# A two-block transformer forward in float32: convolution products in four buffers, delta-rule gating a tile ahead, first level masked by GpSimd, third scores sooner

## The chip, the cores and the metric

The kernel runs on one core of one Trainium2 chip. The metric is the device time of one execution in microseconds (us), the median of several runs. Engine names in the text: TensorE (PE), VectorE (DVE), ScalarE (ACT), GpSimd (POOL), SyncE (SP, which here only issues the loads of weights).

## The reference

Two transformer blocks over one sequence of 512 tokens with 1024 features, all in float32. Reduced to what the change touches:

```python
# block 1, delta rule: per chunk of 64 tokens and per head
lower = b * (k k^T) * dec_strict
sol   = triangular_solve(lower + I, rhs)            # the inverse is built in levels
o     = scan(step, s0, ...)                         # state passed from chunk to chunk
ya    = rmsnorm(o, norm_w) * silu(z)                # the gating of the outputs
# block 1, sparse attention: scores against compressed blocks, selected blocks and a window
p = softmax(q k^T - slope * dist);  yb = sum of gates * (p v)
mixed = (g_a * (ya @ w_a2d) + g_b * (yb @ w_b2d)) @ w_o
# feed-forward with a short convolution, then a per-layer embedding, then block 2:
q, k, v, glu_a, glu_g = split(rms_norm(h) @ w_in)
u = glu_a * sigmoid(glu_g)
u = depthwise_conv(u, 31 taps) + b;  u = silu(layer_norm(u))
h = h + concat(attention(q, k, v), u) @ w_out
# and a second feed-forward
```

## The kernel before

**Weights.** All large products multiply a 128x128 weight block with 512 tokens. A weight arrives as float32 in `RAW[b]` (two buffers), ScalarE rounds it into `WH[b]` (`stage_hi`, L302, tile name whi), VectorE subtracts to get the low half `WL[b]` (`stage_lo`, L309, wlo), and TensorE makes three products per block, high by high, high by low and low by high (`product`, L322 to L324). A piece is up to 16 blocks, so 48 products. `stage_hi(ph, i, b)` waits until TensorE has ended the piece that lies in buffer b and then rounds the piece after the next; TensorE waits for its low half (`weights_ready`). Each engine runs its own list of instructions in the order written; semaphores tie them together. `T` is 4 tiles of 128 tokens.

**First level (gdn_pe, gdn_act, gdn_dve, gdn_pool).** Per tile t, VectorE makes the decayed key-key blocks (L994 to L999, signal `at_ready`), the query-key block (L1003, `qk_done`) and then the start of the inverse, identity minus the entries of level 0: L1005 multiplies `ATC` by the mask `level`, L1006 takes it from `eye` (`tt_ready`). GpSimd scales the queries (L1084, after `qk_done`) and masks the entries of level 1 into `OFFC[1]` (L1077); later it masks those of the levels 2 to 5 into the two buffers in turn. TensorE turns each tile (L679) when `tt_ready` says so, and five levels follow, each as products (L700), copies by ScalarE (L883), products (L708), a subtraction by VectorE (L1011) and turns.

**Gating.** After the recurrence, TensorE turns the outputs of tile t (L790) into bank 4 + t % 2, VectorE multiplies by the gain and the gate into `TMP[t % 2]` (L1067, `yt_ready`), ScalarE takes the high half (L908, `yt_hi`), VectorE the low half (L1070, `yt_lo`). TensorE goes on to the next turn when `yt_ready` of the tile before is there, and, after the last turn and one more such wait, to the rest of the projection "nq".

**Scores of block 1 (nsa_pe, nsa_dve).** A pair p of heads goes through scores on TensorE (L1219), `top(p)` on VectorE (bias and maximum, L1380), the exponential on ScalarE (L1338), `factors(p)` on VectorE (L1388, L1389), scaling on GpSimd (L1467), turn, copy and values on TensorE. Pairs 0 and 1 are started ahead of the value projection `nv_pe` (L1132 to L1134); then the compressed scores (L1264) follow, and the loop over `ITER` starts with pair 2.

**Convolution of block 2 (blk2_act, blk2_dve, conv_pool).** 31 taps for each of four channel groups. VectorE sums 73 of the taps (`TAPS`, L2065 and L2068), the other 51 (`LATE_TAPS`) are multiplied by ScalarE (L1986 for a group's first, L1989 for the rest) into a buffer of `PT2` and added by GpSimd (L2199, `last_tap_done`). ScalarE's product k waits for the add of product k - 2, as there are two buffers. This runs beside the projections "glu" (four pieces), "qk2" (four) and "v2" (two): ScalarE does a gate (L1997), a `stage_hi` and five products for each group, then six products and a `stage_hi` for each piece of "qk2", then the rest, then the exponentials. GpSimd scales the probabilities (L2207) after its last add. The tile `PT2` has four parts of 512 columns, of which the products use two.

```python
                    else:
                        act.wait_ge(last_tap_done, k - 1)
                        ins = nc.scalar.mul(PT2[:, 0, k % 2, :], src, w)
...
            for p in range(NPIECE["qk2"]):
                products(6)
                stage_hi(act, "qk2", p // 2, p % 2, p >= 2)
```

## Time and profile before

| what | value |
|---|---|
| median of 3 runs | 1605.27 us (1605.24 to 1605.73) |
| the profiled execution: its own time | 1607.56 us |
| its span | 1605.8 us |
| mean granted clock of TensorE | 0.971 |
| TensorE busy with products | 1529.8 us, 95% |
| VectorE busy | 867.0 us, 54% |
| ScalarE busy | 641.9 us, 40% |
| GpSimd busy | 212.6 us, 13% |

The span is the part of the execution that the profile covers; the time of the same execution is 1.76 us longer, and it is 2.3 us above the median of the other runs. Times in the rows are microseconds from the start of the span, unless marked ns. A granted clock of 1.00 is 2.4 GHz, 0.50 is 1.2 GHz. Products are pipelined, so that one starts about 0.23 us after the one before it although each is listed with 0.39 us.

### The profile page before, as it was taken

To read this page: it belongs to the slowest core of one execution; us is meant where nothing else is said; L and a number is where in the kernel's file an instruction comes from. 1 tells how busy PE (TensorE), PEld (TensorE's weight loads), DVE (VectorE), ACT (ScalarE), POOL (GpSimd) and SP (SyncE) were. 2 spreads that over 40 slices of the span, in tenths; PEclk is the share of its full clock that TensorE was granted. 3 is DMA by queue.
4 is the path that set the end of the run, shared out by engine and by line. 5 is a ranking of instruction groups with operands and counts; after the bars stand their busy time and mean duration, and the time that the engine had idled before them with its cause. 6 is when DMAs were issued, how large, how long until landed. Compare 5 with 4: busy or idle time off the path is not lost. (4 is left out here: it accounts for less than half of the span.)

```text
span 1605.8 us, 21770 instructions
## 1 busy us (share of the span) xinstructions
PE 1529.8 (95%) x8438; PEld 1247.9 (78%) x8438; DVE 867.0 (54%) x1300; ACT 641.9 (40%) x936; POOL 212.6 (13%) x191
## 2 busy tenths in 40 slices
PE   6997999999999899999999998989799999999998
PEld 5777978667888777888888876767578888888886
DVE  5755446673444477766732266677626444444222
ACT  5354422463223244443422155454635444443221
POOL 0004000681000000000000001378610000000000
PEclk9999999999999999999999998999979999999999
DMA  5210032001223313233232233122103223222321
GB/s 211 79 53 16 2 142 101 21 1 40 98 93 110 105 53 103 81 104 104 69 115 90 91 123 105 53 79 79 30 24 105 91 92 104 99 83 73 104 94 71
DMA packets 22534, 132.17 MB, mean 82 GB/s; under 512 B 2480, under 2 KB 2864, under 8 KB 12224
## 3 DMA queue, kind: packets, MB, share of 16 engines
q1 hardware_dynamic: 20672, 123.48, 22.8%
q0 software_dynamic: 928, 6.36, 1.0%
q10 hardware_dynamic: 864, 1.36, 0.2%
q8 instruction: 49, 0.80, 0.2%
q14 instruction: 21, 0.17, 0.0%
HBM read 129.09 MB, written 2.10 MB: 82 GB/s over the span
## 5 line engine op out<-in xcount | busy, mean ns | idle before, releaser
L322 PE MATMUL ps<-AH,whi 128*128 128x512 f32 x1280 | 509.6, 398 | 39.1 <-DVE wlo L309 14.6
L323 PE MATMUL ps<-AL,whi 128*128 128x512 f32 x1280 | 504.8, 394 | 0.0
L324 PE MATMUL ps<-AH,wlo 128*128 128x512 f32 x1280 | 504.3, 394 | 0.0
L309 DVE TENSOR_TENSOR wlo<-raw,whi 128x2048 fp32r<-128x2048 f32 (+3 forms) x124 | 251.2, 2026 | 272.0 <-ACT whi L302 271.8
L322 PEld LDWEIGHTS ps<-AH,whi 128*128 128x128 f32 x1280 | 244.7, 191 | 95.9 <-issue 21.9
L324 PEld LDWEIGHTS ps<-AH,wlo 128*128 128x128 f32 x1280 | 244.3, 191 | 52.0
L323 PEld LDWEIGHTS ps<-AL,whi 128*128 128x128 f32 x1280 | 244.5, 191 | 50.4 <-issue 0.2
L302 ACT ACTIVATE whi<-raw 128x2048 fp32r<-128x2048 f32 (+3 forms) x124 | 210.3, 1696 | 169.9 <-PE ps L324 169.9
L322 PE MATMUL ps<-HH,whi 128*128 128x512 f32 x352 | 136.9, 389 | 0.0
L323 PE MATMUL ps<-HL,whi 128*128 128x512 f32 x352 | 136.9, 389 | 0.0
L324 PE MATMUL ps<-HH,wlo 128*128 128x512 f32 x352 | 136.9, 389 | 0.0
L322 PEld LDWEIGHTS ps<-HH,whi 128*128 128x128 f32 x352 | 66.1, 188 | 13.8
L323 PEld LDWEIGHTS ps<-HL,whi 128*128 128x128 f32 x352 | 66.1, 188 | 13.7
L324 PEld LDWEIGHTS ps<-HH,wlo 128*128 128x128 f32 x352 | 66.1, 188 | 13.6
L2199 POOL TENSOR_TENSOR CU<-CU,PT 128x512 f32<-128x512 f32 x49 | 74.4, 1519 | 15.7 <-ACT PT L1989 9.8
L1467 POOL TENSOR_SCALAR PR<-PR,RL 128x384 f32<-128x384 f32 (+3 forms) x60 | 63.3, 1071 | 12.8 <-DVE RL L1389 12.4
L2246 POOL TENSOR_TENSOR hT<-CG,RR 128x512 f32<-128x512 f32 x2 | 2.5, 1264 | 426.5 <-ACT RR L2241 426.5
L2317 POOL DMA_DIRECT2D XF<-pT x1 | 0.8, 769 | 433.9 <-PE ps L324 433.9
L329 PE MATMUL ps<-ident,PR 128*128 128x128 f32 x224 | 40.6, 302 | 9.1 <-ACT PT L1975 5.2
L1989 ACT ACTIVATE PT<-UG,cols 128x512 f32<-128x512 f32 x49 | 34.5, 719 | 34.8 <-POOL CU L2199 34.8
L329 PEld LDWEIGHTS ps<-ident,PR 128*128 128x128 f32 x224 | 25.3, 147 | 29.2 <-issue 13.8
L2068 DVE SCALAR_TENSOR_TENSOR ps<-UG,cols,ps 128x512 f32<-128x512 f32 x67 | 47.6, 747 | 0.5
(384 smaller groups left out, 1928.9 us busy)
## 6 DMA issues: line engine op xcount, KB each, us to landing
raw<-wstream SPq DMA_DIRECT2D x78, 1024.0 KB, 4.8
raw<-wstream SPq DMA_DIRECT2D x32, 704.0 KB, 4.1
raw<-wstream SPq DMA_DIRECT2D x16, 768.0 KB, 4.3
hT<-xT SPq DMA_DIRECT2D x4, 512.0 KB, 7.9
raw<-wstream SPq DMA_DIRECT2D x4, 512.0 KB, 3.6
W1k<-w1k_d POOLq DMA_DIRECT2D x1, 2048.0 KB, 10.7
W1v<-w1v_d POOLq DMA_DIRECT2D x1, 2048.0 KB, 15.9
BT<-bias_d POOLq DMA_DIRECT2D x1, 1024.0 KB, 5.6
```

The lines of the kernel that those rows point to most:

```text
L302: nc.scalar.activation(WH[b][:, 0:n], RAW[b][:, 0:n], ACT.Copy).then_inc(w_hi_done, 1)
L309: nc.vector.tensor_tensor(WL[b][:, 0:n], RAW[b][:, 0:n], WH[b][:, 0:n].bitcast(F32), ALU.subtract).then_inc(w_lo_done, 1)
L322: nc.tensor.matmul(out_, WH[b][:, w], xh[:, k, :], start=start and k == 0, stop=False)
L323: nc.tensor.matmul(out_, WH[b][:, w], xl[:, k, :], start=False, stop=False)
L324: last = nc.tensor.matmul(out_, WL[b][:, w], xh[:, k, :], start=False, stop=stop and k == n - 1)
L329: return nc.tensor.transpose(out_, x, eye)
L1467: nc.gpsimd.tensor_scalar(x, x, RL[:, p % 4, b:b + 1], None, ALU.mult).then_inc(p_scaled, 1)
L1989: ins = nc.scalar.mul(PT2[:, 0, k % 2, :], src, w)
L2068: ins = vec.scalar_tensor_tensor(to, src, w, acc(c), ALU.mult, ALU.add)
L2199: nc.gpsimd.tensor_tensor(CU[:, c, :], CU[:, c, :], PT2[:, 0, k % 2, :], ALU.add).then_inc(last_tap_done, 1)
L2246: nc.gpsimd.tensor_tensor(hT[:, m, :], OUT_TMP[n], RR[:, :], ALU.mult).then_inc(out_pooled, 1)
L2317: pool.dma_start(PX, pT.rearrange("(c p) s -> p c s", p=P)).then_inc(p_landed, 16)
```

## The change

Four things are changed.

1. Convolution: the products of ScalarE go into four buffers in turn, product k waits for the add of product k - 4; three, seven, six and four products follow the four gates instead of five each; in "qk2" the rounding comes before the six products instead of behind them.
2. First level: GpSimd masks level 0 into `OFFC[0]` as well, ahead of level 1 and of the scaling of the queries, as soon as `at_ready` is there. VectorE makes one subtraction, `eye` minus `OFFC[0]`, a tile later (`first_level`). Counts of `off_ready` move by four; the masks of level 2, which overwrite `OFFC[0]`, wait for `tt_ready`.
3. Gating: VectorE's gate of tile t + 1 is put ahead of the low half of tile t. TensorE does not wait for `yt_ready` after the last turn.
4. Third scores: `scores(2)` is put ahead of the compressed scores, `factors(1)` behind `factors(0)`, and `top(2)` ahead of the low half of the weights of "mix".

```diff
--- before.py
+++ after.py
@@ -692,7 +692,7 @@
             for lev in range(1, LEVELS - 1):
                 for t in range(T):
                     n = 4 * lev + t
-                    pe.wait_ge(off_ready, n - 3)
+                    pe.wait_ge(off_ready, 2 * t + 2 if lev == 1 else n + 1)
                     pe.wait_ge(t_ready, n - 3)
                     pe.wait_ge(tt_ready, n - 3)
                     for h in range(GH):
@@ -736,7 +736,7 @@
                 last.then_inc(kv_ps, 1)
 
             pe.wait_ge(t_ready, 4 * (LEVELS - 1) + 2)
-            pe.wait_ge(off_ready, 4 * (LEVELS - 2) + 1)
+            pe.wait_ge(off_ready, 4 * (LEVELS - 1) + 1)
             for t in range(T):
                 pe.wait_ge(kv_sb, t + 1)
                 for h in range(GH):
@@ -789,7 +789,7 @@
                 for h in range(GH):
                     last = turned(ps[:, 4 + t % 2, h * P:(h + 1) * P], AT[:, t, h, :], ident[:, :])
                 last.then_inc(ot_ps, 1)
-                if t >= 1:
+                if 0 < t < T - 1:
                     pe.wait_ge(yt_ready, t)
 
 
@@ -883,7 +883,7 @@
                     nc.scalar.activation(flat(YC[b, t, :, :]), ps[b, t, 0:GH * HB], ACT.Copy).then_inc(y_sb, 1)
                 if lev < LEVELS - 1:
                     save_t(lev)
-            act.wait_ge(off_ready, 4 * (LEVELS - 2))
+            act.wait_ge(off_ready, 4 * (LEVELS - 1))
             for n, b in enumerate(halves):
                 nc.scalar.activation(TT[b, :, :, n * HB:(n + 1) * HB].rearrange("p t h n -> p (t h) n"),
                                      TTC[b, :, :, :].rearrange("p t h n -> p (t h) n"), ACT.Copy).then_inc(t_ready, 1)
@@ -968,7 +968,12 @@
             dve.wait_ge(gsum_done, 1)
             vec.tensor_copy(flat(GC[:, :, :]), ps[:, 7, 0:16]).then_inc(gc_saved, 1)
             dve.wait_ge(gc_saved, 1)
-            level, eye = (CS[:, CON[x]:CON[x] + HB].unsqueeze(1).to_broadcast([P, GH, HB]) for x in ("level", "eye"))
+            eye = CS[:, CON["eye"]:CON["eye"] + HB].unsqueeze(1).to_broadcast([P, GH, HB])
+
+            def first_level(t):
+                dve.wait_ge(off_ready, 2 * t + 1)
+                vec.tensor_tensor(TTC[:, t, :, :], eye, OFFC[0][:, t, :, :], ALU.subtract).then_inc(tt_ready, 1)
+
             sums = lambda bank: ps[:, bank, :].rearrange("p (t h n) -> p t h n", t=T, h=GH)[:, :, :, 0]
             lo, hi = halves
 
@@ -1001,9 +1006,9 @@
                     decay(t + 2)
                 dve.wait_ge(rows_done, 4 * t + 4)
                 vec.tensor_tensor(flat(QK[:, t, :, :]), ps[:, o + 3, :], flat(QK[:, t, :, :]), ALU.mult).then_inc(qk_done, 1)
-                dve.wait_ge(at_ready, t + 1)
-                own.link(vec.tensor_tensor(TTC[:, t, :, :], ATC[:, t, :, :], level, ALU.mult))
-                vec.scalar_tensor_tensor(TTC[:, t, :, :], TTC[:, t, :, :], -1.0, eye, ALU.mult, ALU.add).then_inc(tt_ready, 1)
+                if t:
+                    first_level(t - 1)
+            first_level(T - 1)
             for lev in range(1, LEVELS - 1):
                 for t in range(T):
                     n = 4 * lev + t
@@ -1058,36 +1063,45 @@
                                   ALU.mult).then_inc(on_ready, 1)
             stage_lo(dve, "z", 0, 1, True)
             dve.wait_ge(z_ready, 4)
+            def output(t):
+                dve.wait_ge(ot_ps, t + 1)
+                vec.scalar_tensor_tensor(TMP[:, t % 2, :].rearrange("p (h n) -> p h n", h=GH),
+                                         ps[:, 4 + t % 2, :].rearrange("p (h n) -> p h n", h=GH), col("gdn"),
+                                         ZS[:, :, t * P:(t + 1) * P], ALU.mult, ALU.mult).then_inc(yt_ready, 1)
+
+            output(0)
             for t in range(T):
+                if t + 1 < T:
+                    if t:
+                        dve.wait_ge(yt_lo, t)
+                    output(t + 1)
+                dve.wait_ge(yt_hi, t + 1)
                 tok = slice(t * P, (t + 1) * P)
-                dve.wait_ge(ot_ps, t + 1)
-                tmp = TMP[:, t % 2, :].rearrange("p (h n) -> p h n", h=GH)
-                if t >= 2:
-                    dve.wait_ge(yt_lo, t - 1)
-                vec.scalar_tensor_tensor(tmp, ps[:, 4 + t % 2, :].rearrange("p (h n) -> p h n", h=GH), col("gdn"),
-                                         ZS[:, :, tok], ALU.mult, ALU.mult).then_inc(yt_ready, 1)
-                dve.wait_ge(yt_hi, t + 1)
-                vec.tensor_tensor(YAL[:, :, tok], tmp, YAH[:, :, tok].bitcast(F32), ALU.subtract).then_inc(yt_lo, 1)
+                vec.tensor_tensor(YAL[:, :, tok], TMP[:, t % 2, :].rearrange("p (h n) -> p h n", h=GH),
+                                  YAH[:, :, tok].bitcast(F32), ALU.subtract).then_inc(yt_lo, 1)
 
         def gdn_pool(pool):
             def offs(lev, t):
                 m = CS[:, CON["level"] + lev * HB:CON["level"] + (lev + 1) * HB].unsqueeze(1).to_broadcast([P, GH, HB])
+                if lev == 2:
+                    pool.wait_ge(tt_ready, t + 1)
                 if lev > 2:
                     pool.wait_ge(y_ps, 4 * (lev - 3) + t + 1)
                 nc.gpsimd.tensor_tensor(OFFC[lev % 2][:, t, :, :], ATC[:, t, :, :], m, ALU.mult).then_inc(off_ready, 1)
 
             nc.gpsimd.memset(ST[:, :, :, :], 0.0).then_inc(state_ready, 1)
             for t in range(T):
+                pool.wait_ge(at_ready, t + 1)
+                offs(0, t)
+                offs(1, t)
                 qd = QKV[:, 0:GH, t * P:(t + 1) * P]
                 pool.wait_ge(row_exp, t + 1)
                 pool.wait_ge(qk_done, t + 1)
                 nc.gpsimd.tensor_tensor(qd, qd, Y1[:, t, :, :], ALU.mult).then_inc(qd_ready, 1)
-                pool.wait_ge(at_ready, t + 1)
-                offs(1, t)
             for lev in range(2, LEVELS - 1):
                 for t in range(T):
                     offs(lev, t)
-            pool.wait_ge(off_ready, 4 * (LEVELS - 2))
+            pool.wait_ge(off_ready, 4 * (LEVELS - 1))
             nc.gpsimd.memset(TT[halves[1], :, :, 0:HB].rearrange("p t h n -> p (t h) n"), 0.0).then_inc(off_ready, 1)
 
 
@@ -1296,10 +1310,11 @@
                                                 W2[:, 2 + f, :], start=f == 0, stop=f == 1)
             last.then_inc(kv_c_ps, 1)
             nv_pe(pe, 1)
+            scores(2)
             pe.wait_ge(kv_c_sb, 1)
             compressed_scores()
             for i in ITER:
-                if i < len(PAIRS):
+                if 2 < i < len(PAIRS):
                     scores(i)
                 if i - 2 < len(PAIRS):
                     turn(i - 2)
@@ -1412,6 +1427,7 @@
             top(1)
             nv_dve(dve, 0)
             factors(0)
+            factors(1)
             dve.wait_ge(kv_c_ps, 1)
             for g in range(NG):
                 for b in range(2):
@@ -1421,11 +1437,12 @@
                                           ps[32 * r:32 * r + NC, 6, (1 + g) * DK:(2 + g) * DK])
             ins.then_inc(kv_c_sb, 1)
             nv_dve(dve, 1)
+            top(2)
             stage2_lo(dve, "nv", 1)
             for i in ITER:
-                if i - 1 < len(PAIRS):
+                if 2 < i < len(PAIRS) + 1:
                     factors(i - 1)
-                if i < len(PAIRS):
+                if 2 < i < len(PAIRS):
                     top(i)
                 if i - 2 < len(PAIRS) and i not in ACT_SAVES_BOTH:
                     save_probs(dve, vec.tensor_copy, i - 2, 0)
@@ -1985,8 +2002,9 @@
                         act.wait_ge(ug_ready, c + 1)
                         ins = nc.scalar.activation(CU[:, c, :], src, ACT.Identity, bias=B2[:, c:c + 1], scale=w)
                     else:
-                        act.wait_ge(last_tap_done, k - 1)
-                        ins = nc.scalar.mul(PT2[:, 0, k % 2, :], src, w)
+                        if k >= 4:
+                            act.wait_ge(last_tap_done, k - 3)
+                        ins = nc.scalar.mul(PT2[:, k // 2 % 2, k % 2, :], src, w)
                     ins.then_inc(prod_ready, 1)
                 del left[:n]
 
@@ -1997,10 +2015,10 @@
                 nc.scalar.activation(SQ[:, b, :], SQ[:, b, :], ACT.Tanh, scale=0.5).then_inc(gate_ready, 1)
                 if c:
                     stage_hi(act, "glu", i, b, i == 1)
-                products(5)
+                products((3, 7, 6, 4)[c])
             for p in range(NPIECE["qk2"]):
+                stage_hi(act, "qk2", p // 2, p % 2, p >= 2)
                 products(6)
-                stage_hi(act, "qk2", p // 2, p % 2, p >= 2)
             products(len(LATE_TAPS))
 
             def probabilities(p):
@@ -2196,7 +2214,7 @@
                 pool.wait_ge(prod_ready, k + 1)
                 if j:
                     pool.wait_ge(last_tap_done, k)
-                    nc.gpsimd.tensor_tensor(CU[:, c, :], CU[:, c, :], PT2[:, 0, k % 2, :], ALU.add).then_inc(last_tap_done, 1)
+                    nc.gpsimd.tensor_tensor(CU[:, c, :], CU[:, c, :], PT2[:, k // 2 % 2, k % 2, :], ALU.add).then_inc(last_tap_done, 1)
                 else:
                     nc.gpsimd.memset(B2[:, c:c + 1], 0.0).then_inc(last_tap_done, 1)
             for p in range(len(PAIRS2)):
```

## Rows read from the trace of the kernel before

**Rows 1.** The page, engines: busy time, share of the span.

```profile
PE 1529.8 (95%) x8438; PEld 1247.9 (78%) x8438; DVE 867.0 (54%) x1300; ACT 641.9 (40%) x936; POOL 212.6 (13%) x191
```

**Rows 2.** Groups by line, 112 to 134: busy us, mean ns, idle before.

```profile
L1006 DVE SCALAR_TENSOR_TENSOR Tm<-Tm,CS 128x256 f32<-128x256 f32 x4 | 5.5, 1376 | 0.1
L1084 POOL TENSOR_TENSOR QKV<-QKV,Y 128x512 f32<-128x512 f32 x4 | 5.2, 1312 | 123.3 <-DVE QK L1003 123.3
L1077 POOL TENSOR_TENSOR OFF<-TT,CS 128x256 f32<-128x256 f32 x5 | 4.3, 864 | 0.0
...
L1005 DVE TENSOR_TENSOR Tm<-TT,CS 128x256 f32<-128x256 f32 x4 | 1.6, 408 | 0.0
```

**Rows 3.** Timelines, 130 to 134: start us, us, instruction, [idle before <- releaser].

```profile
130.99 1.97 PE L679 MATMUL ps<-ident,Tm 64*64 64x64 f32 x32 [5.98 <-DVE AT L999]
133.43 1.12 PE L679 MATMUL ps<-ident,Tm 64*64 64x64 f32 x16 [0.46 <-DVE Tm L1006]
...
131.91 1.38 DVE L1006 SCALAR_TENSOR_TENSOR Tm<-Tm,CS 128x256 f32<-128x256 f32 x1
...
131.69 1.31 POOL L1084 TENSOR_TENSOR QKV<-QKV,Y 128x512 f32<-128x512 f32 x1 [2.08 <-DVE QK L1003]
```

**Rows 4.** Timeline of TensorE, the gating and the product after it.

```profile
216.74 1.04 PE L329 MATMUL ps<-ident,AT 128*128 128x128 f32 x8
...
222.35 0.80 PE L322 MATMUL ps<-AH,whi 128*128 128x512 f32 x1 [1.39 <-DVE TMP L1067]
```

**Rows 5.** Timeline of VectorE, first gate and last low half.

```profile
217.45 0.75 DVE L1067 SCALAR_TENSOR_TENSOR TMP<-ps,cols,ZS 128x512 f32<-128x512 f32 x1 [1.70 <-PE ps L329]
...
225.04 0.69 DVE L1070 TENSOR_TENSOR YAL<-TMP,YAH 128x512 fp32r<-128x512 f32 x1 [0.69 <-ACT YAH L908]
```

**Rows 6.** Windows of 1 us: length, TensorE busy (count), granted clock, DMA share, GB/s.

```profile
221.00:222.00 1.00, 0.00 (x0) 0.50 0.00 0
...
227.00:228.00 1.00, 1.00 (x4) 0.60 0.47 111
```

**Rows 7.** Timeline of TensorE around the third scores.

```profile
289.41 4.12 PE L1264 MATMUL ps<-KC,QT 64*128 64x32 f32 x64
293.34 2.06 PE L1219 MATMUL ps<-KT,QT 64*128 64x512 f32 x4
...
301.38 1.13 PE L1219 MATMUL ps<-KT,QT 64*128 64x512 f32 x4
```

**Rows 8.** Groups by line, the convolution's stretch, 1023 to 1118.

```profile
L2199 POOL TENSOR_TENSOR CU<-CU,PT 128x512 f32<-128x512 f32 x49 | 74.4, 1519 | 15.7 <-ACT PT L1989 9.8
L2068 DVE SCALAR_TENSOR_TENSOR ps<-UG,cols,ps 128x512 f32<-128x512 f32 x58 | 40.8, 747 | 0.5
...
L309 DVE TENSOR_TENSOR wlo<-raw,whi 128x2048 fp32r<-128x2048 f32 x7 | 16.4, 2343 | 13.2 <-ACT whi L302 13.2
L302 ACT ACTIVATE whi<-raw 128x2048 fp32r<-128x2048 f32 x7 | 13.3, 1901 | 0.0
...
L2085 DVE TENSOR_TENSOR TMP<-ps,RR 128x512 f32<-128x512 f32 x4 | 2.7, 683 | 0.1
```

**Rows 9.** Timeline of TensorE: a whole piece, and the two waits for weights.

```profile
1023.56 0.44 PE L322 MATMUL ps<-AH,whi 128*128 128x512 f32 x1
...
1034.32 0.39 PE L324 MATMUL ps<-AH,wlo 128*128 128x512 f32 x1
1036.51 0.61 PE L322 MATMUL ps<-AH,whi 128*128 128x512 f32 x1 [1.81 <-DVE wlo L309]
...
1077.66 0.79 PE L322 MATMUL ps<-AH,whi 128*128 128x512 f32 x1 [6.37 <-DVE wlo L309]
```

**Rows 10.** Timelines: an add beside a subtraction, the last adds, scores 2.

```profile
1034.82 2.77 POOL L2199 TENSOR_TENSOR CU<-CU,PT 128x512 f32<-128x512 f32 x1 [0.54 <-ACT PT L1989]
...
1106.40 11.53 POOL L2199 TENSOR_TENSOR CU<-CU,PT 128x512 f32<-128x512 f32 x7 [0.38 <-ACT PT L1989]
...
1127.20 1.99 PE L1866 MATMUL ps<-KT,QT 64*128 64x512 f32 x8 [0.63 <-DVE V L2113]
```

## The prediction

> **What bounds the kernel now.** I read the page first. Its top says that TensorE is busy for 95% of the span [rows 1], so time can come only from three things: stretches in which TensorE stands still, stretches in which it runs at the lower of its two clock levels, and work taken off it. The change takes no matrix product away, so I looked for standstills and slow stretches next to the edited lines, with the timeline of TensorE, the list of grouped instructions of two stretches, and 1 us windows for the granted clock.
>
> Four places stand out. In the first level of the triangular inverse TensorE waits 5.98 us and then 0.46 us for VectorE [rows 3]. In the gating of the delta rule's output it waits 1.39 us before each of the last steps, and starts the next projection at half clock [rows 4, 6]. At the third scores it runs slowly without waiting [rows 7]. In the convolution it waits 1.81 us and 6.37 us for the low half of weights, both times followed by slow products [rows 9].
>
> **The port.** Before pricing anything I needed to know why L1006 is so slow. L1005 and L1006 have the same 128x256 shape, but one takes 408 ns and the other 1376 ns [rows 2]. At the last tile GpSimd's L1084 runs 131.69 to 133.00 and L1006, started at 131.91, ends at 133.29, just behind it [rows 3]: a VectorE operation that reads two SBUF tensors stands still while a GpSimd operation runs. The reverse shows in the convolution: an add that starts at 1034.82, during the weight subtraction L309, takes 2.77 us [rows 10], where others in the 49 give a pace of about 1.30 + 0.14 us; the 49 average 1519 ns because of it [rows 8]. The Trainium skill says the same of the two engines (SBUF — State Buffer, "Who interferes with whom": a VectorE instruction with two SBUF inputs contends with a GpSimd instruction that reads SBUF, and who starts first keeps the port for the whole instruction). The trace agrees, and its waits are in the terms below.
>
> **First level masked by GpSimd.** Removed from VectorE: four L1005 (0.41 each, 0.44 to the next start) and four L1006 at 1.38, in steps of 1.30 [rows 2]: 4 x 1.74 = 7.0 us. Added: four subtractions of 256 columns; the nearest row is L1005, so 4 x 0.44 = 1.8 us. They read two SBUF tensors, so each can be held by GpSimd. The first is not (it stands right behind the operation that frees GpSimd's next one); the other three come while a mask of their own or the next tile is running, whose length is at most 0.86 us [rows 2]. I take 0.3, 0.3 and 0.6, together 1.2. TensorE is late once (the decay rows of tile 3, because VectorE is now earlier): 0.3 us. Net: 7.0 - 1.8 - 1.2 - 0.3 = 3.7; with the last subtraction waiting only for a mask that is half done it is 4.1. I take 3.9 us; bounds 3.0 (all three held for 0.86) and 4.9 (none held). All of it is on the path: the last tile's turn at 133.43 follows L1006's end by 0.14 us [rows 3]. GpSimd gets four more masks, 4 x 0.86 = 3.5 us, before the last L1084. ScalarE's first copy of a level waits for that L1084; I get its end at about 130.5; the copy needs the level's first products, which follow the turn now at 133.43 by about 2 us, so they come at about 131.5: hidden by 1 us. The clock is no loss: it falls during the long wait and would fall again.
>
> The Trainium skill speaks against this edit (GPSIMD Engine Reference, "Engine selection": elementwise work belongs on VectorE, as GpSimd is about twice as slow with two inputs). The rows agree on the price: 864 ns for a GpSimd mask (part of it waiting) against 408 ns [rows 2]. By that rule the four masks cost 1.8 us more than before; by the rows the extra is on an engine that waits anyway, and the term stays.
>
> **Gating a tile ahead.** Now the loop is a chain: gate on VectorE (0.75), high half on ScalarE, low half on VectorE, next gate; four tiles take 8.3 us [rows 5], and TensorE's turn of tile 3 and then the projection hang on it. After: gates 0 and 1 run back to back, 217.45 to about 218.9, turn 3 needs only gate 1, and no wait on gate 2 follows. The turn runs 218.9 to 219.5 and the projection starts at 219.5 instead of 222.35 [rows 4]: 2.85 us. VectorE ends its last low half at about 223.0 instead of 225.73. Queued behind it are the query copies and the weight subtraction that the next but one piece needs at 236; they are due at 225.6, early enough. GpSimd's loads of the compression weights wait for the last low half, so they also start 2.7 us sooner; TensorE needs them only past 250, no cost.
>
> Then the clock. The stretch from the turns at 216.74 to 222.35 is sparse, the level drops to 0.5 in 221-222 and stays there until 227.6 [rows 6]. Twelve products at 0.43 us instead of 0.23 us (steps in rows 9) lost 2.5 us. With dense work from 219.5, before the point at which the level dropped, I expect it not to drop. Gain 2.5, bounds 0 and 2.5. Together 5.35 us.
>
> **Third scores sooner.** TensorE has no wait here: 64 narrow products in 4.12 us, then scores at half clock, 2.06 us against 1.13 us later at full clock [rows 7]. Moved in front of the narrow ones, behind the dense value projection, the scores run in 1.1 us: 0.9 us less. But the slow stretch begins with the sparse products, which now come later, and it then covers other work of the same density: what is saved at its front may be lost at its end. VectorE's order changes too: factors(1) and top(2) come ahead of a weight subtraction. That weight subtraction queued behind top(2) is 1.3 us later, but is needed only for the mixing gate 80 us on. GpSimd gets pair 1's scaling earlier. I take 0.4 us, bounds -0.5 and 1.5.
>
> **The convolution.** Here three things are chained: ScalarE rounds weights (1.90) and makes products; VectorE subtracts the low half (2.34), reads banks (0.68 a read) and sums taps (747 ns each, in steps of about 0.67, or 0.79 where each needs the one before); GpSimd adds [rows 8]. A TensorE piece of 48 products takes 11.0 us (1023.56 to 1034.32 for 47 steps) [rows 9].
> Step 1. ScalarE does three products instead of five before the second gate, none waiting for an add, so that gate and the rounding come 2.8 us earlier; the low half is done at 1033.7, before TensorE ends its piece at 1034.7. The 1.81 us wait is gone, and the slow start (1.8 us).
> Step 2. From one low half to the next there are then 8 taps (5.4; 6.3 in the first), two bank reads 1.3, the gate on ScalarE, which I estimate at 0.75, the rounding 1.85 and the subtraction 2.2: 11.5 us (12.4 in the first) against 11.0. The low halves come at 1033.7, 1046.0 and 1057.4, where TensorE is ready at 1034.6, 1045.5 and 1057.0: two waits of about 0.5 us.
> Step 3. For the first query piece rounding no longer stands behind six products that each wait for an add (the 6.37 us wait); it is done at 1059.5. What is late next is VectorE, with 8 taps, two copies and four taps: low half done about 1069.2, TensorE ready at 1068.4. Wait 0.9 us. The piece starts at 1069.3 instead of 1077.66, at full clock, which saves another 1.7 us. The later pieces don't wait.
> The sum at the first scores: 1.8 + 1.8 + 6.4 + 1.7, less new waits 0.5 + 0.5 + 0.9, is 9.8; worked step by step it is 10.1. I take 10.1: scores at 1102.1 instead of 1112.2.
> Step 4. GpSimd ends its adds at 1106.40 + 11.53 = 1117.93 now [rows 10]; it stood idle 9.8 us for want of a product [rows 8]. After, I count about 4 us, so 5.6 less, but the subtractions now find it busy and some adds wait 0.4 us longer, four of them: the last add ends at about 1114.0. Scaling of pair 0 (3.1 us) follows to 1117.1. TensorE is ready for that pair's turn at 1115.4, and waits 1.7 us that it doesn't wait now. Scores 2 start at 1118.2 instead of 1127.20 [rows 10]: 9.0. For the chance of a slow stretch after this wait I take 0.4 off: 8.6 us. Bounds: 6.0 (the four subtractions that TensorE waits for held for a whole add, 4 x 0.65 more than half an add) and 10.1 (adds done in time).
> Fresh buffers cost nothing: the other half of that tile is idle here.
>
> **Sum.** 3.9 + 5.35 + 0.4 + 8.6 = 18.25 us. The profiled execution's span was 1605.8 and its time 1607.56, so 1.76 lies around the span: after, 1587.55 and 1589.3. It stands 2.3 us above the median of the runs, so the median goes from 1605.27 to 1587.0.
>
> **Rivals.**
> 1. The clock falls in the gating in spite of the shorter gap, since two short waits remain there: 2.5 us less gained, 1589.5. For it: at 1036.51 a wait of 1.81 us was enough for a slow start [rows 9]. Against: dense work now comes 1.5 us before the drop. 15%.
> 2. The convolution gives back more: GpSimd's adds are held by every subtraction and end at 1117.9 as now; scaling and turn take 4.2 us more, so scores 2 come at 1122.5. Gain there 4.7 less 0.4: 1591.3. 12%.
> 3. GpSimd bounds the first level: per tile two masks, one L1084 and a held subtraction, 0.86 x 2 + 1.31 + 0.44 = 3.5 us against VectorE's 3.2; three tiles, 0.9 us less: 1587.9. Hardly to be told from mine in time, only in the trace. 10%. (The rule of the Trainium skill's GPSIMD Engine Reference quoted above leads here.)
> 4. Slower than before. With rounding ahead of the products ScalarE waits for TensorE's piece (11 us) with at most four products out, 5.7 us of adds: GpSimd may idle 5 us in each of six pieces. Scores 2 would have to come at 1137, after a last add at 1132, to eat the other 9.65 us too; it decides from 18 us of idleness beyond my 4 on. Against: the products that ScalarE makes between two roundings are six, 8.6 us of adds, so a piece leaves 2.4 us idle, not 5. 3%.
> 5. The edits do nothing because other waits take over at once: 1605. 2%.
> The rest, 58%, is my own case, 1584.5 to 1589.5.
>
> **How the numbers follow.** What can be told from no change here is 0.2%, 3.2 us. Only rivals 4 and 5 don't end beyond it: faster 0.95, same 0.02, slower 0.03. Sum of the bounds in the good direction is 1583 (4.9 + 5.35 + 1.5 + 10.1 = 21.9); rival 2 with most of rival 1 is 1593. Range 1583.5 to 1593.
>
> **What would show it.** No 1.8 and 6.4 us waits before L322 in the convolution; its query piece 3 starting 8.4 us sooner after the same start; a new wait of TensorE for GpSimd's scaling before the first turn. The new subtraction ending 3.7 to 4.1 us sooner in the first level, its duration over 0.42 us where it was held. Full clock behind the gating. Wrong would be: a wait in the first level for ScalarE's copy behind L1084, a clock drop behind the gating, or adds that end past 1116 (counted with this stage's shift taken off).

## The result, and the profile after

The changed kernel takes 1582.53 us (median of 4 runs, 1581.71 to 1585.38), the kernel before 1605.5 us beside it: the ratio is 0.9858, 95% interval 0.9841 to 0.9875. I had predicted 1587.0 with a range from 1583.5 to 1593.0, so the kernel is 1 us faster than the fast end of the range. Its profiled execution took 1582.03 us with a span of 1580.2; against the profiled one of before that is 25.5 us, where the sum was 18.25.

Top of the page after, engines first and then the granted clock in 40 slices. TensorE's busy time fell by 11.8 us against [rows 1] though no product was removed: it ran less at the lower level.

```profile
PE 1518.0 (96%) x8438; PEld 1239.6 (78%) x8438; DVE 863.9 (55%) x1296; ACT 641.0 (41%) x936; POOL 217.1 (14%) x195
...
PEclk9999999999999899999999998999889999999999
```

**First level.** Timelines of VectorE, TensorE and GpSimd after, beside [rows 3]. All starts are shifted by about 0.6 us from the loads at the start on.

```profile
122.18 0.41 DVE L975 TENSOR_TENSOR Tm<-CS,OFF 128x256 f32<-128x256 f32 x1
...
125.03 0.56 DVE L975 TENSOR_TENSOR Tm<-CS,OFF 128x256 f32<-128x256 f32 x1
...
128.02 1.43 DVE L975 TENSOR_TENSOR Tm<-CS,OFF 128x256 f32<-128x256 f32 x2
...
127.55 0.69 PE L679 MATMUL ps<-ident,Tm 64*64 64x64 f32 x8 [3.47 <-DVE AT L1004]
...
127.58 1.59 POOL L1090 TENSOR_TENSOR OFF<-TT,CS 128x256 f32<-128x256 f32 x2 [0.19 <-DVE AT L1004]
129.13 1.45 POOL L1100 TENSOR_TENSOR QKV<-QKV,Y 128x512 f32<-128x512 f32 x1
```

The wait of 5.98 us is 3.47 us, the second one of 0.46 is gone. The four subtractions took 0.41, 0.56, 0.56 and 0.94 us (the last two are one line above), where an unheld one takes 0.41. The last three each end 0.27 to 0.29 us behind the end of a GpSimd mask: they are held, and only a little. GpSimd still waits for VectorE (0.19 us), so it doesn't bound the level. The Trainium skill says that a VectorE instruction with two SBUF inputs contends with a GpSimd instruction that reads SBUF (SBUF — State Buffer, "Who interferes with whom"); the trace agrees, with 0.15, 0.15 and 0.53 us as the price here.

**Gating.** Timeline of TensorE, then 1 us windows with all engines (the column behind POOL is the granted clock), beside [rows 4, 6].

```profile
214.11 1.31 PE L329 MATMUL ps<-ident,AT 128*128 128x128 f32 x8 [0.48 <-DVE TMP L1068]
215.19 0.48 PE L322 MATMUL ps<-AH,whi 128*128 128x512 f32 x1
```

```profile
216.00:217.00 1.00, 1.00 (x6) 0.84 (x5) 0.96 (x3) 0.63 (x1) 0.00 (x0) 1.00 0.00 0
...
222.00:223.00 1.00, 1.00 (x7) 0.81 (x6) 0.00 (x0) 0.00 (x0) 0.70 (x2) 1.00 0.82 193
```

One wait of 0.48 us is left, the projection starts with a product of 0.48 us instead of 0.80, and the clock stays at 1.00.

**Third scores.** Timeline of TensorE and 2 us windows, beside [rows 7].

```profile
279.69 1.13 PE L1233 MATMUL ps<-KT,QT 64*128 64x512 f32 x4
280.65 3.66 PE L1278 MATMUL ps<-KC,QT 64*128 64x32 f32 x64
...
285.26 1.13 PE L1233 MATMUL ps<-KT,QT 64*128 64x512 f32 x4
...
289.94 0.63 PE L329 MATMUL ps<-ident,PR 128*128 128x128 f32 x4 [0.44 <-ACT PT L1342]
```

```profile
284.00:286.00 2.00, 2.00 (x18) 1.35 (x16) 1.60 (x3) 1.06 (x2) 0.00 (x0) 1.00 0.52 80
```

No group runs at the lower level any more: the scores take 1.13 us both times, the narrow products 3.66 instead of 4.12.

**Convolution.** Timelines of TensorE and GpSimd, then GpSimd's and ScalarE's groups from 1007 to 1103, beside [rows 8 to 10].

```profile
1030.71 0.50 PE L322 MATMUL ps<-AH,whi 128*128 128x512 f32 x1 [0.26 <-DVE wlo L309]
1053.97 0.50 PE L322 MATMUL ps<-AH,whi 128*128 128x512 f32 x1 [0.76 <-DVE wlo L309]
...
1100.74 0.63 PE L329 MATMUL ps<-ident,PR 128*128 128x128 f32 x4 [0.35 <-POOL PR L2225]
1102.19 0.66 PE L329 MATMUL ps<-ident,PR 128*128 128x128 f32 x4 [0.82 <-POOL PR L2225]
...
1078.73 20.32 POOL L2217 TENSOR_TENSOR CU<-CU,PT 128x512 f32<-128x512 f32 x13 [0.17 <-ACT PT L2007]
1099.03 3.11 POOL L2225 TENSOR_SCALAR PR<-PR,RL 128x512 f32<-128x512 f32 x2
```

```profile
L2217 POOL TENSOR_TENSOR CU<-CU,PT 128x512 f32<-128x512 f32 x49 | 76.3, 1556 | 10.1 <-ACT PT L2007 3.9
...
L2007 ACT ACTIVATE PT<-UG,cols 128x512 f32<-128x512 f32 x49 | 33.4, 716 | 18.4 <-POOL CU L2217 18.2
```

The waits of 1.81 and 6.37 us are gone; 0.26 and 0.76 us stand in their place. GpSimd's adds end at 1099.05; with the 15.1 us by which the stage starts sooner, that is 1114.2 (forecast 1114.0). TensorE's new waits for its scaling (L2225) are there, 1.2 us together (forecast 1.7).

### The profile page after: what moved, and what is told of

The parts are those of the page before. It is cut to its first block and busy times, and to the rows that moved or that the text cites. A ratio compares the mean times of both kernels' runs of the same rounds, so it can differ in the third digit from the quotient of the medians.

```text
span 1580.2 us, 21770 instructions
## 1 busy us (share of the span) xinstructions
PE 1518.0 (96%) x8438; PEld 1239.6 (78%) x8438; DVE 863.9 (55%) x1296; ACT 641.0 (41%) x936; POOL 217.1 (14%) x195
## 5 line engine op out<-in xcount | busy, mean ns | idle before, releaser
L322 PEld LDWEIGHTS ps<-AH,whi 128*128 128x128 f32 x1280 | 242.7, 190 | 85.9 <-issue 21.4
L2217 POOL TENSOR_TENSOR CU<-CU,PT 128x512 f32<-128x512 f32 x49 | 76.3, 1556 | 10.1 <-ACT PT L2007 3.9
L1353 ACT ACTIVATE PR<-ps,NM 128x384 f32<-128x384 f32 (+3 forms) x60 | 30.5, 513 | 27.3 <-DVE NM L1395 27.2
```

What stands on the lines that cost most here:

```text
L322: nc.tensor.matmul(out_, WH[b][:, w], xh[:, k, :], start=start and k == 0, stop=False)
L1353: nc.scalar.activation(probs(p, b)[:, 0:n], ps[:, u % 4, 0:n], ACT.Exp, bias=NM[:, u % 4, :], scale=-1.0, accum_out=LS[:, p % 4, b:b + 1]) ...
L2217: nc.gpsimd.tensor_tensor(CU[:, c, :], CU[:, c, :], PT2[:, k // 2 % 2, k % 2, :], ALU.add).then_inc(last_tap_done, 1)
```

## The experiments

Where an experiment's trace gains or loses is read from one difference: the start of an instruction there less the start of the same instruction in the trace of before. The table gives how this difference changes over seven stretches (named by before's times) and its value at the end; below 0 is sooner. The last columns are the runs.

| kernel | 110-140 | 216-230 | 230-288 | 288-330 | 370-380 | 1007-1127 | 1127-1200 | end | median, us (runs) | before beside it |
|---|---|---|---|---|---|---|---|---|---|---|
| changed | -3.85 | -5.63 | +0.05 | -2.59 | -2.47 | -9.16 | -1.40 | -25.8 | 1582.53 (4) | 1605.50 |
| a_again, the same | -4.21 | -5.63 | 0.00 | -2.58 | -2.50 | -9.13 | -1.53 | -27.6 | 1585.75 (4) | 1607.28 |
| a_more, the same | -4.06 | -5.62 | +0.03 | -2.59 | -0.87 | -9.07 | -1.17 | -24.0 | 1585.41 (4) | 1607.41 |
| a_last, the same | -4.25 | -5.62 | +1.59 | -2.58 | -0.90 | -9.08 | -1.20 | -24.5 | 1584.76 (4) | 1606.85 |
| b_again, before | -0.05 | -1.06 | +1.66 | +1.08 | -2.49 | +1.27 | -1.61 | -2.7 | 1605.08 (1) | 1607.28 |
| s_first | -3.78 | -1.22 | +1.66 | -0.38 | +0.37 | +0.54 | +0.29 | -2.6 | 1601.52 (12) | 1606.36 |
| s_gate | -0.25 | -5.62 | +1.63 | -0.74 | -0.96 | -0.08 | +0.77 | -6.7 | 1600.81 (6) | 1606.36 |
| s_third | -0.12 | +0.27 | +0.01 | -2.55 | -2.46 | +1.19 | +0.61 | -4.5 | 1602.97 (12) | 1606.36 |
| s_conv | +0.12 | +0.24 | +0.01 | -0.22 | -2.47 | -9.17 | -1.19 | -12.9 | 1595.66 (6) | 1606.36 |
| s_order | -0.23 | +0.03 | +0.05 | +0.01 | 0.00 | -8.76 | -1.22 | -10.8 | 1596.03 (4) | 1607.28 |
| a_2buf | -4.28 | -5.62 | +1.54 | -2.59 | -0.91 | -8.67 | +0.63 | -22.0 | 1584.27 (4) | 1605.61 |
| a_nothird | -3.86 | -5.61 | +0.02 | +0.12 | -0.14 | -9.14 | -1.15 | -19.9 | 1585.59 (4) | 1607.28 |
| a_nothird2 | -4.16 | -5.62 | +1.63 | +0.48 | -0.90 | -9.28 | -0.60 | -20.7 | 1588.22 (4) | 1607.41 |
| v_pe | -4.07 | -5.62 | +0.03 | -0.76 | +0.13 | -9.32 | -0.48 | -20.1 | 1587.90 (4) | 1606.85 |
| v_dve | -4.04 | -5.62 | +1.65 | +4.05 | +0.05 | -9.31 | -0.57 | -13.4 | 1590.05 (4) | 1606.85 |
| f_glu | -3.68 | -5.62 | +1.46 | -2.58 | -0.92 | -9.10 | -1.15 | -22.6 | 1585.40 (4) | 1607.41 |
| f_att2 | -4.27 | -5.63 | +1.60 | -2.58 | -0.88 | -9.10 | -1.20 | -24.7 | 1582.11 (5) | 1607.41 |
| f_att2b | -4.08 | -5.62 | +1.59 | -2.58 | -0.88 | -9.16 | -1.03 | -23.9 | 1583.98 (5) | 1606.85 |
| f_five | -4.38 | -5.63 | +1.49 | -2.60 | -0.93 | -9.22 | -1.42 | -25.5 | 1582.15 (5) | 1605.61 |

### The four parts, each alone

Each is the kernel before with one of the four changes, the diff here in short: s_first `first_level` and GpSimd's masks of level 0; s_gate `output(t + 1)` a tile ahead and the last wait gone; s_third the moved `scores(2)`, `factors(1)`, `top(2)`; s_conv buffers and order.

```diff
 s_first: -own.link(level mask)     +first_level(t - 1)
 s_gate:  -if t >= 1:              +if 0 < t < T - 1:
 s_third: +scores(2)  (ahead of compressed_scores)
 s_conv:  -products(5)             +products((3, 7, 6, 4)[c])
```

> The kernel before with the first level's edit alone (masks of level 0 on GpSimd, VectorE only subtracts). Theory A (each part is worth its own waits and its own slow stretch, and the parts add): the wait of 5.98 us before the first level is 3.5 us and the place is left 4.5 to 4.8 us sooner; time 4.5 us below before. Theory B (what exceeded the forecast comes from slow stretches elsewhere, which depend on all shifts together): the shift at the end of the span differs from that behind the first level by 2 us or more, because a slow stretch further on comes or goes. The drop at 371 to 378 us stays in A and may go in B.

> The kernel before with the gating's order alone. Theory A: 5.4 to 5.6 us gained behind the gating (2.9 of waits, the rest because TensorE's clock no longer falls in 221 to 228), the same 5.5 us at the end; the drops at 292 to 300 and 371 to 378 us stay. Theory B: one of these two goes as well and 2.4 us or more come on top, 7.5 to 10 us in all.

> The kernel before with the third scores and their factors moved alone. Theory A: the drop at 292 to 300 us and that at 371 to 378 us both go with this edit, since they lie in the stage that it reorders: 2.5 us gained by 316 us, 4.9 to 5.0 us by 380 us and at the end. Theory B (the recorded term of 0.4 us was right for this edit alone, and the rest came with the earlier shift of the stage): 0 to 1 us gained by 316 us, the drop at 371 us stays, at most 1 us in all.

> The kernel before with the convolution's edits alone (four product buffers, rounding ahead of the products). Theory A: 9.3 us sooner at the scores of pair 2 relative to the start of the stage, 10.4 us at the end of the span with the short drop at 1132 to 1136 us gone. Theory B: in the stage the same 9.3 us, but the slow stretches behind it fall elsewhere, and the end differs from 10.4 us by 1.5 us or more, either way.

Ratios: s_first 0.9967 (0.9957 to 0.9978), s_gate 0.9960 (0.9946 to 0.9975), s_third 0.9981 (0.9972 to 0.9990), s_conv 0.9939 (0.9922 to 0.9956). The medians lie 4.8, 5.6, 3.4 and 10.7 us below before, together 24.5, beside 21.5 to 23.0 for the changed kernel in its four comparisons. So the parts add within the width of their intervals, as theory A says, and each shows its gain in its own stretch. Two expectations of theory A fell: s_third was to gain 4.9 to 5.0 us at the end and its runs gained 3.4, and s_conv ends 12.9 us sooner instead of 10.4, as B said. s_conv edits nothing ahead of 1000 us and yet is 2.47 us sooner in 370-380. Timelines of TensorE, before and then s_conv:

```profile
371.09 0.40 PE L329 MATMUL ps<-ident,PR 128*128 128x128 f32 x1 [0.30 <-POOL PR L1467]
371.42 0.70 PE L1246 MATMUL ps<-PT,V 128*64 128x128 f32 x4
...
373.54 2.08 PE L1255 MATMUL ps<-CP,VB 128*128 128x128 f32 x8
```

```profile
371.17 0.30 PE L329 MATMUL ps<-ident,PR 128*128 128x128 f32 x1 [0.30 <-POOL PR L1467]
371.40 0.44 PE L1246 MATMUL ps<-PT,V 128*64 128x128 f32 x4
...
373.22 1.16 PE L1255 MATMUL ps<-CP,VB 128*128 128x128 f32 x8
```

From 320 to 371 us both start the same instructions within 0.1 us of each other; then one falls to the lower level and the other doesn't. (Further ahead they differ by up to 1 us, since the slow stretch at 293 us is shorter in s_conv.)

### Twice the same kernel

> The kernel before once more, unchanged, for its trace. The kernel with the convolution's edit alone showed full clock at 371 to 378 us although nothing ahead of 1000 us was edited in it. Theory C: which of the slow stretches behind sparse work appear differs from one execution to the next, so that this trace differs from the first one in at least one of the stretches at 220, 292, 371, 1132 and 1190 us, with starts of instructions ahead of it that agree within 0.5 us. Theory A (a slow stretch belongs to the schedule): the same stretches, all fourteen within 1 us.

> The changed kernel once more, for a narrower interval and a second trace. Theory A: 1582.5 us, 23.8 us below before, and no slow stretch between 134 and 538 us again. Theory C: the same median within 1.5 us, but one slow stretch of those that were absent (220, 292 or 371 us, counted in the time of before) is there in this trace, or one at 1133 to 1154 us is shorter.

b_again bears out theory C. a_again doesn't by itself: its trace has none of the absent stretches, as theory A said, and its median of 1585.75 us lies 3.2 above the first one's, further than either theory allowed. But a_more has a slow stretch at 360 us, and a_last one at 237 and one at 360, that the first two traces of the changed kernel lack. Windows of 2 us in the first trace of before and then in b_again:

```profile
224.00:226.00 2.00, 2.00 (x7) 1.52 (x6) 1.31 (x3) 1.58 (x2) 0.00 (x0) 0.50 0.00 0
...
250.00:252.00 2.00, 2.00 (x11) 1.64 (x10) 1.97 (x4) 0.00 (x0) 0.00 (x0) 1.00 0.81 197
...
374.00:376.00 2.00, 2.00 (x10) 1.90 (x10) 0.00 (x0) 0.00 (x0) 0.00 (x0) 0.50 0.00 0
```

```profile
224.00:226.00 2.00, 2.00 (x9) 1.62 (x8) 2.00 (x4) 0.90 (x1) 1.02 (x2) 0.87 0.03 8
...
250.00:252.00 2.00, 2.00 (x6) 1.55 (x6) 1.97 (x4) 0.00 (x0) 0.00 (x0) 0.55 0.38 160
...
374.00:376.00 2.00, 2.00 (x14) 1.78 (x14) 0.00 (x0) 0.00 (x0) 0.00 (x0) 1.00 0.04 8
```

The slow stretch behind the gating is shorter in b_again, one at 250 is new, the one at 374 is missing. The 62 runs of the kernel before reach from 1603.4 to 1609.9 us (median 1606.5), the 16 of the changed one from 1580.2 to 1589.1 (median 1584.9). The first measurement's 1582.53 is the lowest of four medians; pooled, the change is worth 21.6 us. That the spread comes from the clock is in part argued: over the 16 runs the time falls as the mean granted clock rises (0.982 in the fastest, 0.976 in the slowest), but only one run of each set of four has a trace. The Trainium skill puts the point at which the level changes down to where the work falls in a count of the chip's own that doesn't start with the kernel (TensorE: Matmul & The Clock Gate, "What's actually happening"); the traces agree, as far as two executions with equal starts and unequal levels can show it.

### The third scores, put back and halved

a_nothird and a_nothird2 are the changed kernel without `scores(2)` ahead, `factors(1)` and `top(2)`; v_pe undoes VectorE's lines alone, v_dve TensorE's alone (each with its condition in the loop).

```diff
 v_pe:             v_dve:
-factors(1)       -scores(2)   (ahead of compressed_scores)
-top(2)
```

> The changed kernel with the third scores, factors and top put back to their place of before. Theory A (the edit keeps the clock up in its stage): a slow stretch is back at about 282 to 290 us and the time is 2.5 to 3.4 us longer than the changed kernel's, 1585 to 1586 us. Rival (the slow stretch there had gone because the gating's edit shifted the stage): no slow stretch there, and the time within 1 us of the changed kernel's.

> The changed kernel without the third scores' edit, a second time. Theory: slow stretches at about 282 to 290 us and 360 to 370 us as in its first trace, 2.5 to 5 us longer than the changed kernel. Rival: one of the two stretches is missing here, and the medians differ by less than 1.5 us.

> The changed kernel a third time, beside the same kernel without the third scores' edit, for more runs of both. Theory (the third scores' edit is worth 2.5 us and more): this kernel's median is 2.5 to 5 us below that of the kernel without it. Rival (the recorded 0.4 us, on the mean over executions): the two medians within 1.5 us. Nearly no slow stretch between 134 and 538 us in this trace under the theory; one of two traces has one under the rival.

> The changed kernel with VectorE's half of the third scores' edit undone (factors(1) and top(2) back behind the weight subtraction); TensorE still takes scores(2) ahead of the narrow products. Theory (the order on TensorE alone keeps its clock up, since the scores follow the dense value projection and the narrow products stand in their place): no slow stretch at 280 to 290 us, 2.6 us gained between 288 and 316 us of before's time, time as the changed kernel's within 1 us. Rival (VectorE's sooner factors close waits of TensorE in 286 to 294 us and that keeps it up): the slow stretch is back, and the time is 2.5 us longer.

> The changed kernel with TensorE's half of the third scores' edit undone (scores(2) back behind the narrow products); VectorE keeps its new order. Theory: the slow stretch of 6.8 us at 282 to 290 us is back and nothing is gained there, 2 to 3 us slower than the changed kernel. Rival: no slow stretch, 2.6 us gained all the same. VectorE stands at top(2) until those scores come, so the weight subtraction behind it is late by some 4 us in either case, and is needed only much later.

Timeline of TensorE in v_dve and then in v_pe:

```profile
281.83 3.76 PE L1278 MATMUL ps<-KC,QT 64*128 64x32 f32 x64
285.43 1.74 PE L1233 MATMUL ps<-KT,QT 64*128 64x512 f32 x4
...
295.70 0.60 PE L329 MATMUL ps<-ident,PR 128*128 128x128 f32 x3 [1.99 <-ACT PT L1341]
```

```profile
280.59 3.66 PE L1278 MATMUL ps<-KC,QT 64*128 64x32 f32 x64
...
285.20 1.13 PE L1233 MATMUL ps<-KT,QT 64*128 64x512 f32 x4
...
290.09 0.63 PE L329 MATMUL ps<-ident,PR 128*128 128x128 f32 x4 [0.65 <-ACT PT L1342]
```

All ten traces with the whole edit gain 2.55 to 2.60 us in 288-330, and none has a slow stretch there; all nine without TensorE's half (before's two among them) have one. v_pe has none either, and gains 2.34 us by 316, before a slow stretch at 306 to 310 us takes 1.58 back. So TensorE's order is what removes the slow stretch at the scores. In its runs, though, v_pe misses its expectation (within 1 us of the changed kernel): 1587.90 us, against 1584.76 for a_last beside it. Its slow stretch at 306 us isn't explained by waits, since those ahead of it are the same in a_more, which has none there. Window of v_pe, then the longest such wait in v_pe and in a_more:

```profile
306.00:308.00 2.00, 2.00 (x19) 1.67 (x18) 0.33 (x2) 0.60 (x3) 2.00 (x2) 0.57 0.04 8
```

```profile
304.13 0.63 PE L329 MATMUL ps<-ident,PR 128*128 128x128 f32 x4 [1.07 <-ACT PT L1342]
```

```profile
303.41 0.63 PE L329 MATMUL ps<-ident,PR 128*128 128x128 f32 x4 [1.05 <-ACT PT L1342]
```

Whether VectorE's half is worth something by itself stays open. v_dve is worse in this stretch than doing nothing: VectorE stands at `top(2)` for scores that come late, and TensorE then waits 1.99 us for probabilities and has two more slow stretches, at 296 and 313 us; it loses 4.05 us there. In time the edit is worth about 2.5 us: 1587.4 (median of 8 runs without it) against 1584.9. This is less sure than the traces: the ranges of runs overlap (1583.2 to 1589.9 and 1580.2 to 1589.1), and of the two pairs measured side by side one shows 2.8 us (a_nothird2 and a_more) and the other nothing (a_nothird 1585.59, a_again 1585.75), against the expectation of 2.5 to 3.4.

### The convolution's order and its buffers

s_order is before with the order alone and two buffers, a_2buf the changed kernel with two buffers. The diff is a_2buf's against the changed kernel, ScalarE's side; GpSimd's add reads the same part of `PT2`.

```diff
-if k >= 4:
-    act.wait_ge(last_tap_done, k - 3)
-ins = nc.scalar.mul(PT2[:, k // 2 % 2, k % 2, :], src, w)
+act.wait_ge(last_tap_done, k - 1)
+ins = nc.scalar.mul(PT2[:, 0, k % 2, :], src, w)
```

> The kernel before with the convolution's order alone (rounding ahead of the products, 3, 7, 6, 4 and 6 products), still with two product buffers. Theory (the order frees the weights, the buffers only keep the products from waiting): the waits of 1.8 and 6.4 us shrink to under 1 and under 3 us, but each product past the second waits for the add two before it, so gates and roundings are still 1 to 3 us late in each piece; 6 to 8 us gained. Rival (the buffers don't matter): 10 us gained as with both. Other rival (without the buffers the order gives nothing, since ScalarE stands behind the adds all the same): under 3 us.

> The changed kernel with two product buffers again, all else kept. Theory (the order does it, the buffers only let ScalarE run ahead): 0.1 to 0.5 us less gained at the scores of pair 2 (8.7 to 9.1 us from the start of the stage instead of 9.1 to 9.2), time within 1 us of the changed kernel's 1585. Rival (with all edits together the buffers matter): 1 us and more lost between 1007 and 1127 us of before's time.

ScalarE's and GpSimd's groups in s_order, 1007 to 1118:

```profile
L2199 POOL TENSOR_TENSOR CU<-CU,PT 128x512 f32<-128x512 f32 x49 | 75.9, 1548 | 11.0 <-ACT PT L1989 5.1
...
L1989 ACT ACTIVATE PT<-UG,cols 128x512 f32<-128x512 f32 x49 | 34.5, 719 | 35.9 <-POOL CU L2199 35.9
```

With two buffers ScalarE stands 35.9 us before its products instead of 18.4, but nothing on TensorE's path waits behind it: GpSimd's idle time before its adds is 11.0 us against 10.1. The order brings 8.76 of 9.17 us (s_conv), the buffers 0.4 to 0.5. My expectation for s_order (6 to 8 us) was too low, and the rival that the buffers don't matter is nearly right. a_2buf came within 1 us of the changed kernel.

### What a slow stretch costs

The changed kernel keeps a slow stretch of 20 us in the second attention and one of 10 to 14 us at the GLU's norm. Added products that serve nothing (their results are overwritten) fill such places.

```diff
 f_att2, f_att2b, f_five, in scores(p):
+if p >= 11 and b == 0:
+    nc.tensor.matmul(ps[:, s2_bank(p, b), :], ones[:, :], KT2[:, 0, :], start=True, stop=True)
 f_att2, f_att2b: the same once ahead of values(14) and values(15)
 f_glu, the product once ahead of spread_rms(pe, 4) and four times behind it:
+pe.wait_ge(bank_free, RING0["glu"] + 2)
+nc.tensor.matmul(ps[:, ring("glu", 0), :], ones[:, :], E[:, 0, :], start=True, stop=True)
```

> The changed kernel with seven products added that serve nothing (ones by KT2, 128x512 f32, into a scores bank that is free), one ahead of each of the scores 11 to 15 of the second attention and one ahead of the values of pairs 14 and 15. Theory (the long slow stretch of 20.5 us at 1132 to 1154 us is set by how little work TensorE gets there, and its waits leave room): the stretch is gone or at most 10 us long, the first product of the output projection starts 2 to 6 us sooner, and the kernel is 2 to 6 us faster than the changed one in spite of 6 us of added work. Rival (the waits for ScalarE and VectorE set the pace there, the clock is only a symptom): the stretch may go, but the time stays within 1.5 us. Second rival (the clock doesn't follow the work): the stretch stays and the kernel is 3 to 6 us slower.

> The changed kernel with five products added that serve nothing (ones by E, 128x512 f32), one ahead of the spreading of the root before the GLU projection and four behind it, where TensorE waits 1.1 and 3.2 us. Theory (a wait followed by dense work costs its length and a slow start; filling the wait saves the slow start): the stretch of 10.2 us at 976 to 987 us goes or shrinks to 3.4 us, the projection's products run in steps of 0.23 us from the start, 1.5 to 3 us gained. Rival (the projection's first products are paced by VectorE's low halves, so a full clock gives nothing): under 0.7 us. The added products end ahead of the first low half at 981.6 us and delay nothing in either.

> The changed kernel with the seven added products in the second attention, once more. Theory D (the slow stretch costs time in the plain executions): its median again 2 to 4 us below the changed kernel's of the same call. Theory E (as its first trace says, ScalarE's and VectorE's waits set the pace there, and the first difference was a spread between runs): within 1.5 us of it, and in the trace 1.2 us gained from 1127 to 1200 us of before's time, as in the changed kernel.

> The changed kernel, a fourth time, as the measure for the other three. Theory E: 1584 to 1586 us in median, a spread of 3 us or more between its runs, from slow stretches that come and go. Theory D needs it 2 to 4 us above the kernel with the added products.

> The changed kernel with five of the seven added products of the second attention, those ahead of the scores 11 to 15; the two ahead of the last values are left out. Theory (the two last ones cost 1.9 us on the path and the full clock at the mean's products, 3.1 us instead of 5.3, paid for them): the output projection starts 1 to 2 us sooner than in the changed kernel, counted from the scores of pair 2. Rival (without them the clock falls before the mean's products, which take 5 us again): 0 to 0.4 us sooner, and the time within 1.5 us of the changed kernel's 1585.

The same stretch in a_more and then in f_att2, each first in 4 us windows, then in TensorE's timeline with its wait for VectorE and the first product of the output projection.

```profile
1138.00:1142.00 4.00, 3.46 (x20) 1.97 (x18) 2.63 (x13) 2.37 (x12) 2.66 (x4) 0.50 0.62 207
1142.00:1146.00 4.00, 4.00 (x26) 2.58 (x26) 1.01 (x8) 1.60 (x7) 1.97 (x4) 0.50 0.14 57
```

```profile
1147.60 0.69 PE L1907 MATMUL ps<-PT,V 128*64 128x128 f32 x4 [0.89 <-DVE AL L2153]
...
1156.77 0.79 PE L322 MATMUL ps<-AH,whi 128*128 128x512 f32 x1
```

```profile
1138.00:1142.00 4.00, 2.90 (x21) 1.58 (x22) 2.00 (x12) 2.69 (x12) 2.99 (x4) 1.00 0.78 260
1142.00:1146.00 4.00, 3.50 (x30) 1.92 (x28) 1.20 (x9) 1.96 (x9) 2.14 (x4) 1.00 0.03 8
```

```profile
1146.64 0.44 PE L1912 MATMUL ps<-PT,V 128*64 128x128 f32 x4 [1.14 <-DVE AL L2158]
...
1156.12 0.79 PE L322 MATMUL ps<-AH,whi 128*128 128x512 f32 x1
```

The stretch has shrunk from 20.5 to 3.4 us, and in the trace nothing is gained: f_att2 entered this attention 0.64 us ahead of a_more (its other shifts) and leaves it 0.65 ahead. With the full clock TensorE only waits longer, 1.14 for 0.89 us here. f_five leaves it 0.3 us sooner by the same reckoning, so the theory that its two missing products were in the way falls as well. f_glu raises the clock at the projection, whose steps become 0.23 us, and then meets this, from its timeline of TensorE:

```profile
986.73 0.40 PE L324 MATMUL ps<-AH,wlo 128*128 128x512 f32 x1
...
989.27 0.50 PE L322 MATMUL ps<-AH,whi 128*128 128x512 f32 x1 [0.39 <-DVE AL L426]
991.31 0.50 PE L322 MATMUL ps<-AH,whi 128*128 128x512 f32 x1 [0.39 <-DVE AL L426]
```

VectorE's low halves pace it, and its time is the changed kernel's (1585.40 and 1585.41). The added products ran partly at the lower level themselves, and the projection began without a wait behind them, so they may hold it by some tenths. What stays open: the runs with added products in the attention have medians of 1582.1, 1584.0 and 1582.2. All 15 together have a median of 1582.2, 2.8 us under the 1584.9 of the changed kernel's 16, a difference no smaller than the one counted for the third scores above, and no trace shows where it comes from. Side by side it is 3.3 us once (f_att2 and a_more), which is what the theory of f_att2 said, and 0.8 the second time (f_att2b and a_last), which is what theory E said; f_five lies 2.9 us under the 1585 of its expectation, outside the 1.5 of its rival. The traced runs can't decide it, since of the changed kernel's four all were the fastest or second fastest of their set. So the added products are neither a proven gain nor shown to be worth nothing in time.

## Why the prediction was off

**First level, 3.9 us forecast: right.** The four traces of the changed kernel give 3.85 to 4.25, s_first 3.78, all traces with the edit 3.68 to 4.38. The holding of the last three subtractions was forecast as 0.3, 0.3 and 0.6 us and came as 0.15, 0.15 and 0.53. The lower bound of 3.0 doesn't follow from its terms: 7.0 - 1.8 - 3 x 0.86 - 0.3 is 2.3. Rival 3 fell with GpSimd's wait of 0.19 us.

**Gating, 5.35 us forecast: right.** 5.61 to 5.63 in every trace with the edit, of which in the first trace 3.0 are waits (forecast 2.85) and 2.6 the clock (2.5). Part of this depends on which trace of before stands beside it: b_again and s_first lose 1.1 and 1.2 us less there without the edit, as their slow stretch is shorter. Rival 1 fell: no slow stretch follows the turns in any trace with the edit. The one at 236 to 248 us that costs 1.6 us in some (column 230-288) also comes without it, in b_again and s_first.

**Third scores, 0.4 us forecast: the step that failed.** I wrote that what is saved at its front may be lost at its end, since the slow stretch begins with the sparse products and would move with them. It didn't move, it vanished: with the scores taken right behind the dense value projection and the narrow products in the gap, TensorE's granted clock stays at 1.00 there in ten traces of ten, and 2.6 us come instead of 0.4, also beyond my bound of 1.5. A saving of the whole slow stretch was worth weighing as a case, from [rows 7] alone: scores at 2.06 us against 1.13, twice, and narrow products at 4.12.

**Convolution, 8.6 us forecast: the mechanism right, the size short.** The steps hold to tenths: waits of 0.26 us, none and 0.76 for 0.5, 0.5 and 0.9, the first scores 10.0 us sooner (10.1), GpSimd's idle time 5.6 us less (15.7 to 10.1, as forecast), the last add at 1114.2 (1114.0), scores 2 sooner by 9.1 us (9.0). The 0.4 us that I took off for a slow stretch behind the new wait wasn't lost in the four traces of the changed kernel, though a stretch at 1111 us stands in those of a_2buf, a_nothird2 and v_pe, and one at 1119 in v_dve, so that the chance was real. The short one at 1132 to 1136 us of before went, worth another 1.2 us; but b_again lacks it too, so this part isn't the change's. Rival 2 (adds held by every subtraction, the last one ending at 1117.9) fell with the last add at 1114.2, and rival 4 (GpSimd starved) with the 3.9 us for which GpSimd waits for products. The steps take the four buffers for granted (in step 1 no product waits for an add); the runs show that they carry only 0.4 us. The stretch is no fixed measure either: b_again and s_third, without the edit, lose 1.3 and 1.2 us in it against the first trace of before.

**What no step held.** In 370-380 the first trace gains 2.47 us where nothing was edited. It also comes in b_again and s_conv, and not in a_nothird, so most of it is scatter of the clock. A share may still be the third scores': none of the ten traces with that edit whole has this slow stretch at its full 6.8 us, and six of the ten without it do. On the mean the column gives 1.4 us with the edit and 0.6 without; no run isolates this. My sum had no term for such scatter.

**The account.** At the edits: 4.1 + 5.6 + 2.6 + 9.1 = 21.4 us, and the pooled runs say 21.6. From the 1605.27 that the forecast starts from, this gives 1583.9, inside my range. My 18.25 with 2.6 in place of 0.4 is 20.45, which from 1605.27 gives 1584.8. That this is the pooled 1584.9 is in part luck, as the pooled median of before is 1606.5 and not 1605.27. The rest of the distance to 1582.53 goes with the scatter of four runs, for which my range, worked out from bounds of the terms alone, had no room.

## What to carry to other kernels

Price a slow stretch in full only where TensorE itself sets the pace behind it: there half clock cost its whole excess in the traces (gating, third scores), while in a chain paced by other engines it hid in their waits (the norm, the second attention, each by its traces). Where sparse products follow a dense phase, moving denser work in front of them can do away with the slow stretch altogether, as at the third scores, so weigh "it vanishes" as a case of its own. And before pricing the slow stretches of one trace, compare two executions of the same kernel; those that come and go aren't fixed by the schedule alone.

## What the hardware showed that was not expected

Two executions that for 50 us start each instruction within 0.1 us of each other can take different levels from one instruction on (371 us), worth 2.5 us; the same kernel's runs lie up to 6.5 us (before) and 9 us (changed) apart, which such differences would explain. The level also falls where TensorE's longest wait is 0.30 us, if the work between is single 128x128 turns and narrow products. And seven added f32 products of 128x512 in an attention cut its slow stretch from 20.5 to 3.4 us at no cost in time; its trace shows no gain either, while the runs leave one open.
